# RWKV quantities made by token tile between the recurrence's stages, two chunk lanes instead of three

## The reference, cut to what matters

```
xs = p_b + (prev - p_b) * b_mu
r, k, v, wl, al, gl = split_cols(xs, ...)
w_log = -softplus(-(b_w0 + tanh(wl) @ b_w2)) - 0.5 ;  decay = exp(-exp(w_log))
a = sigmoid(b_a0 + al @ b_a2) ;  g = sigmoid(gl) @ b_g2
kk = heads(k * b_kk) ;  kk = kk * rsqrt(sum(kk * kk) + 1e-12)
k = k * (1.0 + (a - 1.0) * b_ka)
# per token: state = state*w + (state @ -kk) (kk*a)^T + v k^T ;  y = state @ r
out = (layernorm(y) + (sum(r * k * b_rk)) * v) * g
```

## Time and profile before

| | us |
|---|---|
| median of 3 runs | 3896.8 |
| the other two runs | 3895.93 and 15196.09 |
| profiled execution | 3896.55 |
| its span | 3894.8 |
| rwkv, first block | 337 to 473 |
| rwkv, second block | 474 to 758 |
| tail | 758 to 3894.8 |

### The profile page before, as it was taken

The page is one execution under the profiler, slowest core; times in us unless marked ns, Lnnn a source line. Parts: engine busy times, 40 slices in busy tenths (PEclk is TensorE's granted clock), DMA queues, the critical chain, the costliest instruction groups (busy, mean ns, idle before and its releaser), DMA issues.

```text
span 3894.8 us, 33849 instructions
## 1 busy us (share of the span) xinstructions
PE 3111.6 (80%) x9394; PEld 1521.5 (39%) x9394; DVE 2702.3 (69%) x6472; ACT 1335.9 (34%) x3949; POOL 1427.4 (37%) x1217
## 2 busy tenths in 40 slices
PE   7866489778877777798989877898898886777777
PEld 4444289643323232244434433333343422322232
DVE  0088645378776666778998857699977667667664
ACT  1134222133333333332557233234552333333332
POOL 0021000045444444455434534454344444444443
PEclk9987599889999999999989999999899999999999
DMA  3100000399999999999989999999999999999998
GB/s 131 34 4 7 0 1 1 118 366 418 416 419 419 420 414 411 415 412 417 392 339 394 396 387 420 419 416 407 354 419 421 421 409 422 421 420 413 415 420 354
DMA packets 210444, 1293.14 MB, mean 332 GB/s; under 512 B 23632, under 2 KB 32848, under 8 KB 62672
## 3 DMA queue, kind: packets, MB, share of 16 engines
q0 software_dynamic: 165888, 1208.03, 75.5%
q1 hardware_dynamic: 44368, 82.96, 5.9%
HBM read 1286.51 MB, written 3.87 MB: 331 GB/s over the span
## 4 chain that ended last, share of the span: by engine, by line
DMA 39%; PE 20%; DVE 10%; issue 7%; ACT 3%; POOL 1%; DVEq 0%; ACTq 0%; POOLq 0%
DMA ring<-in_uv,route 38%; PE banks L1437 14%; DVE ring L1377 4%; DVE X L1387 1%; PE banks L1765 1%; ACT route L1422 1%; POOL ring L1366 1%; PE banks L1825 1%; DVE own L2073 1%; PE banks L1817 1%; ACT route L1407 1%; ACT route L1412 1%; PE banks L1791 1%; DMA own<-in_l_w_out 0%; DMA own<-in_l_peer_wq 0%
## 5 line engine op out<-in xcount | busy, mean ns | idle before, releaser
L1437 PE MATMUL banks<-ring,route 128*128 128x512 f32 (+1 forms) x4088 | 1980.6, 621 | 564.1 <-ACT route L1422 547.1
L1366 POOL DMA_INDIRECT ring<-in_uv,route x1152 | 1330.3, 1155 | 1684.1 <-PE banks L1437 1497.5
L1377 DVE SCALAR_TENSOR_TENSOR ring<-ring,XN 128x1024 f32<-128x1024 f32 x1152 | 1409.7, 1224 | 726.6 <-DMA ring<-in_uv,route 718.1
L1437 PEld LDWEIGHTS banks<-ring,route 128*128 128x128 f32 (+1 forms) x4088 | 723.8, 188 | 1650.7 <-issue 831.3
L1407 ACT ACTIVATE route<-route 128x2 f32<-128x2 f32 x576 | 117.6, 204 | 1868.8 <-DVE ring L1377 1868.4
L1422 ACT ACTIVATE route<-IDN,route 128x128 f32<-128x128 f32 x894 | 309.5, 387 | 4.0 <-PE banks L1437 2.8
L1412 ACT ACTIVATE route<-route 128x1 f32<-128x1 f32 x1152 | 276.9, 287 | 23.7 <-ACT route L1407 0.7
L1765 PE MATMUL banks<-own,QP 128*128 128x512 f32 (+1 forms) x400 | 177.8, 568 | 3.7 <-ACT QP L1856 2.2
L1387 DVE SCALAR_TENSOR_TENSOR X<-ring,route,X 128x1024 f32<-128x1024 f32 x130 | 166.5, 1281 | 0.9
L111 POOL TENSOR_TENSOR ys<-ys,IDN 128x4 f32<-128x4 f32 x9 | 9.1, 1009 | 388.6 <-DVE ys L1114 388.6
L1407 ACT ACT_TABLE_LOAD x106 | 136.0, 1283 | 1.9
(11 more groups left out here) (451 smaller groups left out, 3496.8 us busy)
## 6 DMA issues: line engine op xcount, KB each, us to landing
ring<-in_uv,route POOLq DMA_INDIRECT x1152
own<-in_l_w_in SPq DMA_DIRECT2D x16, 1024.0 KB
own<-in_l_w_out SPq DMA_DIRECT2D x12, 1024.0 KB
own<-in_l_peer_wq SPq DMA_DIRECT2D x12, 1024.0 KB
ring<-in_l_w_in SPq DMA_DIRECT2D x2, 2560.0 KB, 21.6
X<-in_x_prompt SPq DMA_DIRECT2D x8, 512.0 KB, 7.4
ring<-in_l_w_out SPq DMA_DIRECT2D x2, 2048.0 KB, 10.2
ring<-in_l_peer_wq SPq DMA_DIRECT2D x1, 4096.0 KB, 16.0
```

The source lines that it names most:

```text
L1366: pool.indirect_dma_start(self.ring[:, s % RING, :], None, self.io[f"uv{of_slot(s)[0]}"], bass.IndirectOffsetOnAxis(ap=self.EI[:, g % 2, k ...
L1377: dve.scalar_tensor_tensor(u, u, 1.0, self.XN[:, of_slot(s)[1], :], ALU.mult, ALU.mult, accum_out=self.HD[:, g % 2, k:k + 1]).then_inc(sel ...
L1437: m = pe.matmul(self.bank[1 + half][0:n, :], self.DG[:, (V_TENSOR[s] - 1) % 4, 0:n], self.ring[:, s % RING, D + 512 * half:D + 512 * half ...
```

## The change

One block in place of two. The quantities are made by token tile t (128 tokens, two chunks; the last has 64) for all 4 head pairs at once, by `pe_tile`, `act_tile` and `dve_tile`, whose pieces are put between the stages of the chunks by a number each. They are kept plain (not as blocks) in small buffers, and ACT spreads each chunk's into the block form (`act_stage` with k = -1) just before its stage 0. Stages 0 and 1 multiply 192 columns instead of 256; the last 64 of them are an identity and give the transposes that stages 2 and 6 made apart, and ACT copies those out of PSUM once DVE has taken its part. DVE applies the masks to the diagonal blocks alone, half of the partitions at a time. There are two lanes instead of three, and a chunk begins every 9 steps instead of every 6. Tile t + 1 is made while chunks 2t and 2t + 1 run. The output weights' load is queued once the last tile is done.

```diff
-def rwkv(nc, io, sb, sig, bank, CST, IDN, wide, side, PA, PB, OBT, X):
...
-        LANES = 3
...
-        NS, LAG, PRODUCTS = 18, 6, 17
...
-        turns = [(c, tau - LAG * c) for tau in range(LAG * last + NS) for c in range(NCH) if 0 <= tau - LAG * c < NS]
...
+LANES, LAG, STAGES = 2, 9, 18
+FIRST, AHEAD = 14, 15
+def rwkv(nc, io, sb, sig, bank, pairs, CST, IDN, wide, side, PA, PB, OBT, X):
...
+    def chunk_turns(eng_stages):
+        return [(FIRST + LAG * c + k, 0, c, k) for c in range(NCH) for k in eng_stages]
+    def tile_turns(when):
+        return [(FIRST - AHEAD + 2 * LAG * t + x, 1, t, name) for t in range(NT) for name, x in when]
+    pe_turns = sorted(chunk_turns(range(0, STAGES)) + tile_turns((
+        ("lora", 3.2), ("sums", 6.4), ("bonus", 12.2), ("turn_v", 12.4))), key=lambda x: x[:2])
+    act_turns = sorted(chunk_turns(range(-1, STAGES)) + tile_turns((
+        ("lora_in", 2.6), ("lora_out", 3.8), ("exps", 5.6), ("sqrt", 6.6), ("v_copy", 13.2))), key=lambda x: x[:2])
+    dve_turns = sorted(chunk_turns(range(0, STAGES)) + tile_turns((
+        ("shift", 0), ("mix", .8), ("add", 1.6), ("squares", 3), ("scan", 4.6), ("decayed", 6.2), ("v_blocks", 7),
+        ("norm", 8), ("key", 9), ("blocks", 10), ("bonus", 11), ("out", 13))), key=lambda x: x[:2])
...
+    def dve_tile(dve, ch, t, name):
...
+        if name == "shift":
+            if t:
+                dve.wait_ge(d5.h, d5.at(t))
+                dve.wait_ge(za.h, za.at(t))
+            before()
+            ch.add(tt(mixed(t, 0, BT), previous(t), now(t), ALU.subtract))
+        elif name == "mix":
+            before()
+            ch.add(tt(mixed(t, 0, BT), mixed(t, 0, BT), lead(V_MU, BT), ALU.mult))
+        elif name == "add":
+            before()
+            tt(mixed(t, 0, BT), mixed(t, 0, BT), now(t), ALU.add).then_inc(sh.h, 1)
+        elif name == "squares":
+            dve.wait_ge(sh.h, sh.at(t + 1))
+            before()
+            ch.add(tt(k4(KK), K, lead(V_KK, 4), ALU.mult))
+            before()
+            tt(KQ[:, f], KK[:, f], KK[:, f], ALU.mult).then_inc(d2.h, 1)
...
+        elif name == "norm":
+            dve.wait_ge(rt.h, rt.at(t + 1))
+            ch.add(dve.reciprocal(KQ[:, f], KQ[:, f]))
+            before()
+            ch.add(dve.scalar_tensor_tensor(KK[:, f], KK[:, f], -1.0, KQ[:, f], ALU.mult, ALU.mult))
+            before()
+            ch.add(tt(RHS[t % 2][:, 0:chunks[t], :, 0, :], by_chunk(k4(KK)), by_chunk(k4(T0)), ALU.mult))
...
+    def pe_stage(pe, c, k):
+        lane, w = c % LANES, work[c % LANES]
+        t, i = c // 2, c % 2
+        b = w.b
+        if k == 16:
+            return
+        if count(c, k):
+            pe.wait_ge(taken[lane].h, taken[lane].at(2 * count(c, k)))
+        if k in (0, 1):
+            if k == 0:
+                pe.wait_ge(spread.h, spread.at(c + 1))
...
+    def act_stage(act, c, k):
+        lane, w = c % LANES, work[c % LANES]
+        t, i = c // 2, c % 2
+        b = w.b
+        halves = [(slice(64 * h, 64 * h + 64), slice(64 * h, 64 * h + 64)) for h in range(2)]
+        if k == -1:
+            act.wait_ge(ready.h, ready.at(t + 1))
+            if c < LANES:
+                act.wait_ge(zc.h, zc.at(3))
             else:
+                produced(act, c - LANES, 15)
+            for q, o in halves:
+                for a in range(2):
+                    act.activation(w.AR[q, :, a, o], RHS[t % 2][q, i, :, a, :], ACT.Copy)
+                act.activation(w.BB[q, :, o], BS[t % 2][q, i, :, :], ACT.Copy)
+                ins = act.activation(w.KB[q, :, o], KS[t % 2][q, i, :, :], ACT.Copy)
+            ins.then_inc(spread.h, 1)
+            return
+        if k in (0, 1):
...
+    def dve_stage(dve, ch, c, k):
...
+        if k == 0:
+            if c == 0:
+                dve.wait_ge(masked.h, masked.at(2))
+            for q, o in halves:
+                for dst, a, mask in ((w.Dg, 0, mask16), (w.O, 0, maskO), (w.M1, 1, maskI)):
+                    ins = tt(dst[q, :, o], w.both[q, :, 64 * a:64 * a + 64],
+                             mask[q, o].unsqueeze(1).broadcast_to([64, 4, 64]), ALU.mult)
+                    if not (a and o.start):
+                        ch.add(ins)
+        elif k == 1:
+            for q, o in halves:
+                for a, mask in ((0, maskS), (1, maskI)):
+                    ins = tt(w.M2[q, :, a, o], w.both[q, :, 64 * a:64 * a + 64],
+                             mask[q, o].unsqueeze(1).broadcast_to([64, 4, 64]), ALU.mult)
+                    if not (a and o.start):
+                        ch.add(ins)
+        elif k == 2:
+            for q, o in halves:
+                ins = tt(w.Dt[q, :, o], b[0][q, 0:256].rearrange("p (q n) -> p q n", q=4),
+                         mask16L[q, o].unsqueeze(1).broadcast_to([64, 4, 64]), ALU.mult)
+                ch.add(ins)
+            before()
+            ins = tt(w.ID, w.Dg, ident.unsqueeze(1).broadcast_to([P, 4, P]), ALU.add)
...
+        @block.sync
+        def _(sp):
+            sp.dma_start(BV[:, :], io["bvec"]).then_inc(loaded.h, 16)
+            sp.wait_ge(zc.h, zc.at(1))
+            for dst, src in ((W2A[0:64, 0, :], io["b_w2"]), (W2A[64:P, 1, :], io["b_a2"]), (G2, io["b_g2"])):
+                sp.dma_start(dst, src).then_inc(gl.h, 16)
+            sp.wait_ge(d5.h, d5.at(NT))
+            WO = Room(wide).take(KD, D)
+            wv = io["l0_w_out"].rearrange("(k p) n -> p k n", p=P)
+            for i in (1, 0):
+                k = slice(4 * i, 4 * i + 4)
+                sp.dma_start(WO[:, k, :], wv[:, k, :]).then_inc(wl[i].h, 16)
+            sp.wait_ge(st_sig.h, st_sig.at(last))
+            sp.dma_start(io["out_b_wkv_p"], ST[:, :, :]).then_inc(stored.h, 16)
+            produced(sp, last - 1, 15)
+            sp.wait_ge(stored.h, stored.at(16))
+            sp.dma_start(ST[:, :, :], io["wkv_t"]).then_inc(loaded.h, 16)
+            sp.wait_ge(st_sig.h, st_sig.at(NCH))
...
```

782 lines of the change are left out of this document (377 added, 405 removed).

## The result

The changed kernel takes 3910.1 us in the median of 6 runs (3907.0 to 3919.2), the kernel before 3897.0 beside it: a ratio of 1.0036, with a 95% interval of 1.0025 to 1.0047. (One of the six runs of the kernel before took 15196 us, which the median hardly feels.) The time lies in the range (3838 to 3942), but on the other side of the kernel before than the forecast of 3889.

A forecast was written before the change was run, and what follows sets the result against it. DVE was taken to bound the first rwkv block, PE the second, DMA the untouched tail. Head, steps and end summed to 397.9 us, plus 16 for the clock, against 420.9: 7 us gained, 3889 us, range 3838 to 3942.

The forecast's parts named there:

- Tile 0 alone: Start of the block: making the first tile before chunk 0 is spread, booked at 38.1 us.
- Small DVE operations 5, of which 3 are in doubt: Part of the head: VectorE's small operations booked at 5 us, 3 of them uncertain after one of 3.51 us.
- norm, key, blocks 9.2: Last item of the head's sum: VectorE's norm, key and blocks for tile 0, 9.2 us.
- Its last nine stages alone, at half clock: 34: End of the block: chunk 8's last nine stages, 25.3 us from stage 13 and four stages of about 2.2.
- chunk 8 without a tile 33: Near the end: chunk 8's first nine steps, with no tile being made beside them, 33 us.
- The walk: Nine steps with two chunks followed through PE, DVE and ACT at full clock: even chunk 35.2 us, odd 38.6.
- My 2 us for the clock: Loss from PE's clock falling in pauses: 2 us per nine steps, 16 in all, between 0 and 7.7 each.
- no row shows 71% held for long: Clock term: PE would be busy 52.6 of 73.8 us, and no profile row showed the clock at such a share.
- DVE's sum for two chunks and a tile: VectorE's work for two chunks and a tile, about 54.5 us, so busy some 73% in the walk.
- The clock neither fell and stayed: Rival, chance 0.22: PE's clock falls and stays down; at 0.79, 39 us slower, 3936 us.
- Running ahead: Rival, chance 0.1: engines run ahead of the steps, each chunk costs DVE's sum of 27.2 us; 3803 us.
- The tiles' work lies cheaper: Rival, chance 0.2: half operations overlap in stages 0 to 2, no clock lost, chunks 0 and 8 at full clock; 3844 us.

The follow-up runs named there:

- e5: Changed kernel with VectorE's small operations behind tile 0's scan, only the two mask products staying in front; 3902.6 us.
- e2: Changed kernel with v's rotation and its copy placed behind the spreading and stage 0, for all tiles; 3909.8 us.
- e8: e7 with v's rotation and its copy placed behind the spreading for all tiles; 3886.4 us.
- e9: e7 with v's rotation and its copy placed behind the spreading for tile 0 alone; 3881.0 us.
- e7: e5 with e4's useless matmuls, and six more behind each of stages 6 to 16 of the last chunk and stage 15 of the one before; 3883.8 us.
- e4: Changed kernel with useless matmuls (dummies) added on PE behind stages 0 to 3 to fill its pauses; 3901.7 us.
- e13: Changed kernel with key in norm's place on VectorE and norm behind the older chunk's stage 12, no dummies; 3899.6 us.
- e14: Changed kernel without the reciprocal of the keys' norm, keys scaled by 0.001 times the norm instead, no dummies; 3890.6 us.
- e3: Kernel before the change with two lanes nine steps apart instead of three lanes six apart, its first block kept; 3970.5 us.

## Why the prediction was wrong, step by step

**The step that failed is "Tile 0 alone", 38.1 us, measured 51.4.** It is 13.3 of the 22 us between sum and measurement. Two things in it. "Small DVE operations 5, of which 3 are in doubt": they took 11.9 (340.29 to 352.22), because GpSimd's memsets, 11.1 us of them in one run, held a tensor_scalar for as long as they ran; e5 takes 12.3 us off the head by order alone. And the sum ended with "norm, key, blocks 9.2", as if the spreading followed blocks; in ACT's order v_copy stands between, behind bonus and rotation at half clock, 7.3 us (382.55 to 389.85). e2, e8 and e9 each took 7 us from the head by that. The rest of the head was right: from tile 0's first pass to its last product 30.3 us were measured for 30.5, and the table of vectors came after 1.8 us for 2.6. Both could be read before: the first from the 3.51 us of L805 and the memset that ended with it, the second from the numbers of the turns (FIRST - AHEAD + 13.2 = 12.2 for v_copy of tile 0, FIRST - 1 = 13 for the spreading of chunk 0).

**"Its last nine stages alone, at half clock: 34" and "chunk 8 without a tile 33" were 5.5 too small** together, 2.5 and 3.0 with the clock's 2. A stage of eight matmuls is 2.93 us at half clock with its reader, not 2.2, which for four stages is the first of these; the clock is down before chunk 8 is alone, which fits the second and isn't shown to be all of it. e7's dummies took 8.7 us off that part.

**The walk held.** Its 306.8 us with the clock were 310.1, no step shorter than booked without the clock: the first, chunk 0 alone, 40.9 for 37, the three full odd ones 42.0, 39.7 and 41.1 for 38.6, the two full even ones 35.6 and 37.5 for 35.2. With the clock up (e4, 0.95 to 1.00) an even step was 36.1 for 35.2, an odd one 38.1 to 39.4 for 38.6. That norm sets the odd step through stage 12 is shown by e13 and e14, and e14 says that the reciprocal's price is more than the walk's 3.4: with the clock it is 5 to 6. My 2 us for the clock was a choice between 0 and 7.7, and at least 12 us over eight steps, 1.5 each, was measured: right in size by choice, not by working. The sentence "no row shows 71% held for long" overlooked one near it: from 474 to 504 us PE was busy 67% of 30 us and had 0.71. The walk's mechanism was right, and so was the main sign named for it (norm in front of stage 12); the chunks end 35.2 to 41.5 us apart in turn, 35 to 39 foretold. DVE's sum for two chunks and a tile was too large: 54.5 us, 50.7 measured from 472.83 to 548.09, so that it was busy 67% there and not 73%.

**The rivals.** The clock neither fell and stayed (0.86 over the steps, 0.84 to 0.96 in each of those with two chunks) nor stayed up. Running ahead did not occur: a chunk takes 38.8 us, far from DVE's sum of 27.2, and e3 shows that a chain of two lanes alone needs 35.9. "The tiles' work lies cheaper" was partly so (the six half-partition operations of stage 0 took 2.22 us, 0.37 each, not 0.44), by 0.4 us a chunk in stage 0: much too small to matter. The table load took 1.28 us with 0.01 to 0.02 us on either side in the changed kernel too, against the 2.66 that the prediction quotes from the Trainium skill's page "ScalarE: Activation LUTs", section "What ACT_TABLE_LOAD costs". Its timeline at 510.6 us:

```profile
510.64 0.40 ACT L1066 ACTIVATE own<-ring 64x256 f32<-64x256 f32 x1
511.05 1.28 ACT L886 ACT_TABLE_LOAD   x1
...
512.35 0.63 ACT L886 ACTIVATE ring<-ring 128x512 f32<-128x512 f32 x1
```

With the head as measured, the same sum would have been 427.2 us, 6 more than the 420.9 before, and with the end 432.7. The head's miss alone turns the sign; steps and end together (8.8 us) would have brought the sum to 422.7, level with before. In the head I had followed what depends on what, and not the order in which each engine's operations stand.
